# Dilated attention: values projected by columns with the weights stationary, then transposed

## The reference, cut to what matters

```python
qb = proj[..., C_QB:C_KB].reshape(b, s, DIL_HEADS, DIL_HEAD_DIM)
kb = proj[..., C_KB:C_VB].reshape(b, s, DIL_HEADS, DIL_HEAD_DIM)
vb = proj[..., C_VB:C_GA].reshape(b, s, DIL_HEADS, DIL_HEAD_DIM)
for gi, (window, dil) in enumerate(DIL_GROUPS):      # (128, 1), (512, 4), (2048, 16)
    hs = slice(gi * 4, gi * 4 + 4)
    o_g, lse_g = _dilated_group(qb[:, :, hs], kb[:, :, hs], vb[:, :, hs], group_bias[gi], dil, window // (2 * dil))
```

## Time and profile before

| | us |
|---|---|
| median of 3 runs (lowest, highest) | 3520.5 (3517.79, 3520.65) |
| the profiled execution's own time | 3523.53 |
| its span in the profile | 3521.7 |
| PE busy, share of the span | 3352.3, 95% |
| DVE busy | 1436.9, 41% |
| ACT busy | 1012.6, 29% |
| mean granted TensorE clock (1 is 2.4 GHz) | 0.978 |

### The profile page before, as it was taken

One profiled execution on the slowest core, in us unless ns is written; L12 is line 12 of the kernel. 1 busy time (PEld: TensorE's weight loads), 2 busy tenths in 40 slices (PEclk: granted clock), 3 DMA queues, 4 the chain that ended last, 5 costly groups with the idle time before them and its releaser, 6 DMA issues.

```text
span 3521.7 us, 38556 instructions
## 1 busy us (share of the span) xinstructions
PE 3352.3 (95%) x16143; PEld 2523.5 (72%) x16143; DVE 1436.9 (41%) x2030; ACT 1012.6 (29%) x2281; POOL 363.3 (10%) x433
## 2 busy tenths in 40 slices
PE   8999999989989999999989999999999999998997
PEld 5566656656656569989873488888888887777876
DVE  3354545455553112112013334444444477532452
ACT  3333342333342123222230024111111233313452
POOL 0121222222231100000001000000000011001111
PEclk9999999999999999999999999999999999997998
DMA  3111010110011011110135222111111131101010
GB/s 140 62 48 42 25 54 34 40 39 24 22 39 37 33 40 37 37 39 29 53 114 195 99 114 70 54 48 48 48 49 52 61 123 36 48 36 55 25 36 25
DMA packets 55565, 194.83 MB, mean 55 GB/s; under 512 B 7232, under 2 KB 14912, under 8 KB 42336
## 3 DMA queue, kind: packets, MB, share of 16 engines
q1 hardware_dynamic: 54528, 191.29, 15.2%
q10 hardware_dynamic: 864, 1.09, 0.1%
HBM read 158.37 MB, written 33.98 MB: 55 GB/s over the span
## 4 chain that ended last, share of the span: by engine, by line
PE 86%; DVE 6%; ACT 5%; issue 1%; DMA 1%; POOL 1%; SPq 0%; ACTq 0%; POOLq 0%; DVEq 0%
PE ps L557 15%; PE ps L2153 14%; PE ps L2154 14%; PE ps L2155 14%; PE ps L1853 4%; PE ps L2030 3%; PE ps L1492 3%; PE ps L632 2%; PE ps L626 2%; PE ps L3031 2%; PE ps L1570 1%; DVE ar L1003 1%; PE ps L638 1%; PE ps L669 1%; PE ps L1535 1%
## 5 line engine op out<-in xcount | busy, mean ns | idle before, releaser
L2153 PE MATMUL ps<-r,r 128*128 128x512 f32 (+4 forms) x2080 | 760.9, 366 | 18.9 <-DVE ar L2682 4.0
L557 PE MATMUL ps<-ar 128*128 128x512 f32 x1408 | 666.5, 600 | 3.4 <-ACT ps L762 2.0
L2154 PE MATMUL ps<-r,r 128*128 128x512 f32 (+3 forms) x1760 | 616.9, 350 | 0.0
L2155 PE MATMUL ps<-r,r 128*128 128x512 f32 (+3 forms) x1616 | 587.9, 364 | 0.0
L2153 PEld LDWEIGHTS ps<-r,r 128*128 128x128 f32 (+2 forms) x2080 | 428.8, 206 | 74.6 <-issue 9.0
L2154 PEld LDWEIGHTS ps<-r,r 128*128 128x128 f32 (+1 forms) x1760 | 368.5, 209 | 38.3 <-issue 5.7
L557 PEld LDWEIGHTS ps<-ar 128*128 128x128 f32 x1408 | 246.4, 193 | 198.6 <-issue 195.9
L2155 PE MATMUL ps<-r 128*128 128x512 f32 (+2 forms) x976 | 352.8, 361 | 0.0
L2155 PEld LDWEIGHTS ps<-r,r 128*128 128x128 f32 (+1 forms) x1616 | 313.2, 194 | 47.0
L2154 PE MATMUL ps<-r 128*128 128x512 f32 x832 | 324.3, 390 | 0.0
L2155 PEld LDWEIGHTS ps<-r 128*128 128x128 f32 (+1 forms) x976 | 211.0, 216 | 20.0
(11 more groups left out here) (316 smaller groups left out, 4452.0 us busy)
## 6 DMA issues: line engine op xcount, KB each, us to landing
ar<-wst SPq DMA_DIRECT2D x102, 1024.0 KB, 4.8
ar<-x SPq DMA_DIRECT2D x16, 512.0 KB, 10.1
ar<-sc_g SPq DMA_DIRECT2D x32, 256.0 KB, 5.0
sc_h<-ar SPq DMA_DIRECT2D x32, 256.0 KB, 2.0
sc_x<-ar SPq DMA_DIRECT2D x16, 512.0 KB, 3.2
ar<-sc_x SPq DMA_DIRECT2D x16, 512.0 KB, 3.9
sc_b<-ar SPq DMA_DIRECT2D x24, 260.0 KB, 2.0
ar<-sc_b SPq DMA_DIRECT2D x3, 2080.0 KB, 21.4
```

Source lines behind the costliest of these rows:

```text
L557: o = t.do.matmul(bk, wv[:, kt, c:c + 128], hT[:, kt, 512 * hf:512 * hf + 512], start=(kt == 0), stop=(kt == 7))
L2153: t.do.matmul(o, l[0], r[0], start=first, stop=False)
L2154: t.do.matmul(o, l[0], r[1], start=False, stop=False)
L2155: return t.do.matmul(o, l[1], r[0], start=False, stop=last)
```

## The change

The values of all three groups are made by `pe_cols`, as queries and keys are: 8 banks a group (four blocks `ct` of 128 channels, two halves `hf` of 512 positions), 24 matmuls each, two steps of 12 to a bank. ACT copies a bank to a new tile `Vs` (128 channels x 1024 positions), writing it in the group's order (residue by residue). When both halves are in, PE transposes the chunks out of `Vs` into bank 7, in three turns for groups 0 and 1 and two for group 2 (`V_TURNS`), one turn at the end of each of the next steps, and DVE copies each turn to `Vt[g]`. The last turns of a group stand in steps of their own. A turn waits for the eviction to `Vs` and for DVE's copy of the turn before; the eviction of a first half waits for the last turn of the block before. So that `Vs` has room, the biases of group 2 go to the place of group 0's and are loaded after its last logits, one output buffer goes over constants that are dead by then, and the gates' buffers move.

```diff
-        Ob = [A(o + 520 * i, 520) for i in range(2)]
-        bias = [A(gates0, 4, 256), A(BIAS1, 4, 256), A(BIAS1 + 1024, 4, 128)]
+        Ob = [A(C0 + 128, 520), A(o, 520)]
+        BIAS1 = o + 520
+        bias = [A(gates0, 4, 256), A(BIAS1, 4, 256), A(gates0, 4, 128)]
+        VS0 = BIAS1 + 1024
+        Vs = A(VS0, 1024)
-        def sp_skew(sp):
-            for n in range(12):
+        def sp_skew(sp, first, last):
+            for n in range(first, last):
-        v_keys = lambda g: [("v", g, sl, i) for sl in range(2) for i in range(len(chunks(g)))]
+        v_keys = lambda g: [("v", g, ct, hf) for ct in range(4) for hf in range(2)]
+        V_TURNS = [[slice(1, 5), slice(5, 8), slice(0, 9, 8)], [slice(1, 12, 3), slice(0, 12, 3), slice(2, 12, 3)], [slice(0, 4), slice(4, 8)]]
+        v_turn_keys = [("v", g, ct, k) for g in range(3) for ct in range(4) for k in range(len(V_TURNS[g]))]
-        plan_dil = [[("v", 0)] * 19,
-                    merged((("att", 0), 34, 0.0, 1.0), (("v", 1), 25, 0.0, 1.0)), [("qk", 1)] * 33,
-                    merged((("att", 1), 34, 0.0, 1.0), (("v", 2), 17, 0.0, 1.0)), [("qk", 2)] * 33,
+        plan_dil = [[("v", 0)] * 20,
+                    merged((("att", 0), 34, 0.0, 1.0), (("v", 1), 20, 0.0, 1.0)), [("qk", 1)] * 33,
+                    merged((("att", 1), 34, 0.0, 1.0), (("v", 2), 20, 0.0, 1.0)), [("qk", 2)] * 33,
-        gbst = [A(gates0 + 512 * i, 512) for i in range(2)] + [A(BIAS1 + 512 * i, 512) for i in range(2)]
+        gbst = [A(BIAS1 + 512 * i, 512) for i in range(4)]
@@ pe_cols
             for kt in range(8):
+                if n >= NS:
+                    t.wait_ge(turned_lo if kt % 2 else turned_hi, ("round", kt))
@@ pe_v
+            def turn(ct, k):
+                t.wait_ge(dil_ev, ("v", g, ct, 1))
+                i = v_turn_keys.index(("v", g, ct, k))
+                if i:
+                    t.wait_ge(norm_out, v_turn_keys[i - 1])
+                for j, (a, m) in enumerate(chunks(g)[V_TURNS[g][k]]):
+                    o = t.do.transpose(q4(bank(7), j)[0:m, :], Vs[:, a:a + m], ident)
+                o.then_inc(*turned.tick(("v", g, ct, k)))
+            turns = len(V_TURNS[g])
+            for ct in range(4):
+                s = 0
+                for hf in range(2):
+                    for _ in pe_cols(t, ("v", g, ct, hf), VW0[g] + ct // 2, ct % 2, hf):
+                        if ct and s < turns:
+                            turn(ct - 1, s)
+                        s += 1
+                        yield
+            for k in range(turns):
+                turn(3, k)
+                yield
@@ pe_att
-                t.wait_ge(dil_ev, v_keys(g)[-1])
+                t.wait_ge(norm_out, ("v", g, 3, len(V_TURNS[g]) - 1))
@@ act_v
+            def part(ct, hf):
+                key = ("v", g, ct, hf)
+                n = 512 // dil
+                a.wait_ge(dil_mm, key)
+                i = v_turn_keys.index(("v", g, ct, 0))
+                if i:
+                    a.wait_ge(turned, v_turn_keys[i - 1])
+                dv = Vs.rearrange("p (r l) -> p l r", r=dil)[:, n * hf:n * hf + n, :]
+                sv = bank(dil_ev.keys.index(key) % 2).rearrange("p (l r) -> p l r", r=dil)
+                a.do.activation(dv, sv, ACT.Copy).then_inc(*dil_ev.tick(key))
+            for ct in range(4):
+                if ct:
+                    part(ct - 1, 1)
+                yield
+                if ct % 2:
+                    act_w_split(a, VW0[g] + ct // 2 + 1)
+                yield
+                yield
+                part(ct, 0)
+                yield
+            part(3, 1)
+            yield
@@ dve_att
-                v.wait_ge(bias_set, 11)
+                v.wait_ge(bias_set, 11 if g == 2 else 7)
@@ dve_v
+            def turned_part(ct, k):
+                v.wait_ge(turned, key)
+                if g == 2:
+                    v.wait_ge(att_mm, (0, 7, "u"))
+                v.do.tensor_copy(Vt[g][0:m, which, 128 * ct:128 * ct + 128], bank(7)[0:m, 0:128 * n].rearrange("p (c n) -> p c n", c=n)).then_inc(*norm_out.tick(key))
+            for ct in range(4):
+                for s in range(4):
+                    if ct % 2 and s == 1:
+                        dve_w_split(v, VW0[g] + ct // 2 + 1)
+                    yield
+                    if ct and s < turns:
+                        turned_part(ct - 1, s)
+            for k in range(turns):
+                yield
+                turned_part(3, k)
@@ sp_qk
+            if g == 1:
+                sp.wait_ge(att_sum, (0, 7))
+                sp_skew(sp, 8, 12)
@@ sp_v
-                yield from idle(n)
-                sp.wait_ge(dil_mm, ("v", g, sl, n - 1))
+                yield from idle(9)
+                sp.wait_ge(dil_mm, ("v", g, 2 * sl + 1, 1))
@@ before the dilated stage
-            sp_skew(sp)
+            sp_skew(sp, 0, 8)
```

More of the change, by code:

```diff
@@ L1322, in program @@
         o += 2048
-        Ob = [A(o + 520 * i, 520) for i in range(2)]
-        o += 1040
-        BIAS1 = o
-        bias = [A(gates0, 4, 256), A(BIAS1, 4, 256), A(BIAS1 + 1024, 4, 128)]
-        assert BIAS1 + 1536 <= NAR
+        Ob = [A(C0 + 128, 520), A(o, 520)]
[3 more added lines that the diff above has]
+        Vs = A(VS0, 1024)
+        assert VS0 + 1024 <= NAR
         bias_set = flow("bias_set", range(12), 16)
-        def sp_skew(sp):
-            for n in range(12):
+        def sp_skew(sp, first, last):
+            for n in range(first, last):
                 g, hh = divmod(n, 4)
@@ L1605, in act_v @@
         def act_v(a, g):
+            dil = DIL[g]
             if g == 0:
                 act_h_round(a)
[L1608 to L1617, removed]
+            def part(ct, hf):
[20 more added lines that the diff above has]
+            yield
         def act_att(a, g):
@@ L1727, in dve_v @@
                 dve_h_round(v)
[L1728 to L1731, removed]
+            def turned_part(ct, k):
+                key = ("v", g, ct, k)
+                which = V_TURNS[g][k]
+                m = chunks(g)[which][0][1]
+                n = len(chunks(g)[which])
+                v.wait_ge(turned, key)
+                if g == 2:
+                    v.wait_ge(att_mm, (0, 7, "u"))
+                v.do.tensor_copy(Vt[g][0:m, which, 128 * ct:128 * ct + 128], bank(7)[0:m, 0:128 * n].rearrange("p (c n) -> p c n", c=n)).then_inc(*norm_out.tick(key))
+            turns = len(V_TURNS[g])
+            for ct in range(4):
[8 more added lines that the diff above has]
+                turned_part(3, k)
         def dve_gb(v, _):
@@ L1751, in sp_v @@
         def sp_v(sp, g):
-            n = len(chunks(g))
             for sl in range(2):
-                yield from idle(n)
-                sp.wait_ge(dil_mm, ("v", g, sl, n - 1))
+                yield from idle(9)
+                sp.wait_ge(dil_mm, ("v", g, 2 * sl + 1, 1))
                 w_load(sp, VW0[g] + sl + 2)
@@ L2006, in program @@
         x_saved = flow("x_saved", [(n, i) for n in (1, 2) for i in i8], 16)
-        norm_out = flow("norm_out", [("h2", i) for i in i8] + [("m", 0)] + [("u", i) for i in i8])
+        norm_out = flow("norm_out", v_turn_keys + [("h2", i) for i in i8] + [("m", 0)] + [("u", i) for i in i8])
         turned, turned_hi, turned_lo = [flow(n, before + [("h2", i, hf) for i, hf in i8h] + [("m", 0, hf) for hf in range(2)] + [("u", i, hf) for i, hf in i8h])
-                                        for n, before in (("turned", []), ("turned_hi", split_keys(0)), ("turned_lo", split_keys(1)))]
+                                        for n, before in (("turned", v_turn_keys), ("turned_hi", split_keys(0)), ("turned_lo", split_keys(1)))]
         def pe_rows(t):
```

## The result

The changed kernel takes 3500.9 us, median of 4 runs (3500.1 to 3502.5), against 3520.0 of the kernel before: ratio 0.9947, 95% interval 0.9930 to 0.9965. It is faster, by 19 us or half a per cent, where 41 us were forecast, and it lies 0.9 us above the range. The profiled execution took 3500.55 us, 19 us more than the 3481.8 forecast for it.

A forecast was written before the change was run, and what follows sets the result against it. PE's stream of matmul starts was taken to bound the kernel. 3523.5 - 49.5 gained + 7.8 for the clock = 3481.8 us for the profiled execution; the median, 3.0 lower, 3479, range 3456 to 3500.

The forecast's parts named there:

- the range: Whole kernel: 3456 us (no falls, two thirds of waits) to 3500 us (nine falls, half the transposes' far bound); chance 0.87.
- What goes and what comes: Dilated stage: strided 256-column value matmuls go; 192 matmuls a group and 116 transposes at 0.1 us each come.
- the sum: PE work of the first values phase and two merged attention phases, without waits: falls by 93.8 us.
- The waits: PE idle behind late evictions and copies: 2.6 us in first values phase, 22.4 and 19.3 in the merged attention phases.
- the walk: Following PE, DVE and ACT queues in the diff's order with traced durations, to find each PE wait in the dilated stage.
- The clock: TensorE's clock falls behind three of four gaps of 3.3 to 3.6 us, 2.6 us of work each: 7.8 us charged.
- The clock's bound of 23.4 us: Upper bound of the clock charge: falls behind all nine gaps of 2.2 us or more.
- The 5.8 us held for dearer transposes: Part of the range's upper end: half the 11.6 us more if the values' transposes took 0.2 us each.
- The rival of the clock: Merged attention phases: 26 small waits keep PE mostly at 1.2 GHz, +85 us there, 3604 us in all; chance 0.03.
- Edits at no cost: Earlier weight loads, later bias DMAs, ACT's regrouped copies, DVE's copies and added waits in `pe_cols`: no cost beyond counted PE waits.

The follow-up runs named there:

- the joined version: Changed kernel with attention and value steps reordered tile by tile, and each phase's last turns put between the next phase's first steps: 3430.1 us, ratio 0.9748.
- the filled kernel: Changed kernel with idle 128 x 512 matmuls put on PE just ahead of its waits for late evictions and copies: 3478.9 us, ratio 0.9887.

## Why the prediction was wrong

- **What goes and what comes, right.** The old values' price was the strided stationary operand: A0 lost 21.6 us of work without it. V0 came to 50.7 us for 50.8. Transposes cost 0.11 us for 0.1. Without waits and at clock 1.00 the whole is worth 90.5 us in the joined version, for 93.8 in the sum, so that the sum put the work 3.3 us too low.
- **The waits, right in place, a little long.** A0 has 18.1 us of idleness for 22.4, A1 15.2 for 19.3. The engines named are those of the walk. Slower matmuls probably cover part of what was walked at full clock; no run separates that.
- **The clock, the step that failed.** "I charge three of them with the fall shown, 7.8 us": that a gap can cost clock was right, which gaps do it and how often was not. From the earlier trace rows it was argued that only the four gaps over 3.3 us would do it. No gap in A0 or A1 was that long, and the longest, 3.07 us, had no fall. There were 11 falls, ten of them behind gaps of 1.5 to 2.8 us. Work grew by 14.1 us in A0 and 17.3 in A1, 8.5 us less was idle, and phases 3 and 5 took 3.9 us longer: 26.8 us net, and with 7.8 charged that is the 19 us between the forecast and the profiled execution. Less the 3.3 us of work put too low, some 23.5 us are the clock's where 7.8 was charged, 2.1 us a fall for the 2.6 taken. If the waits were simply walked too long, it is more: up to 32 us by the clock columns of A0, phase 3, A1 and phase 5, 2.9 a fall.
- **The range.** The clock's bound of 23.4 us was just reached, but by luck: it was made of nine falls behind gaps of 2.2 us and more, and there were 11, six of them behind shorter ones. On top came the 3.3 us of work, and the 3.0 us by which the median was expected below the profiled execution; it came 0.3 above. The 5.8 us held for dearer transposes covered most of that, and the time ended 0.9 us over the range.
- **The rival of the clock** had the right mechanism at too high a dose. It needed 19 falls to be slower than before; there were 11. What the Trainium skill says under "A second HAM failure mode: psum-queue depth-cycling" ("TensorE: Matmul & The Clock Gate"), micro-idles between groups that make the clock oscillate, fits A0 and A1 with their 11 falls.
- **Edits at no cost, right.** The moved biases and buffers measure 0.9998, and no wait of PE in A0, A1 or phases 3 and 5 is named after a weight load or a split.

## What to carry to other kernels

When a change makes steps shorter, write down for each wait what it is queued behind on the other engine, and how much work the new steps put over it; here the old steps of 5.6 us had hidden a chain of 5 to 6 us, and the new ones of 2.8 us did not. Charge TensorE for short gaps twice, once as idleness and once for the clock behind them; before giving up, change the order of the steps, which here took 50.8 us off the stage where the change itself had taken 22.8. Where an idle gap can't be closed, a matmul thrown away in it can pay for itself.

## What the runs showed of the hardware

- A read of the stationary operand with a stride of 4 or 8 elements doubled the distance between starts of 256-column matmuls with 128 held columns: 0.234 us at stride 4 and 0.241 at stride 8, for 0.120 unstrided. With 64 held columns stride 4 cost little (0.118 us for 0.114).
- Between banks of 24 matmuls, a gap of 1.1 us never let the clock fall (0 of 15), one of 2.2 us did in 10 of 15, at 1.5 to 1.6 us each, and one of 3.3 us always, at 1.3 to 2.9 us each. Where attention stands between, one of 3.07 us in A0 did not, one of 1.55 us in A1 did, and in the filled kernel one of 0.76 us did.
- Sixteen float32 transposes or eight float32 matmuls in a gap of 2.2 us kept the clock at 1.00, behind 15 gaps of each kind.
- Idle float32r matmuls put into gaps took 16.9 us off the stage, and 22 us off the median.
